# A float32r block kernel: weights of the gate and up products as the stationary operand

## What is computed

```python
def rmsnorm(x, g):
    xf = x.astype(jnp.float32)
    y = xf * lax.rsqrt(jnp.mean(xf * xf, axis=-1, keepdims=True) + EPS)
    return (y * g.astype(jnp.float32)).astype(x.dtype)

def swiglu(x, w_gate, w_up, w_down):
    return (jax.nn.silu(x @ w_gate) * (x @ w_up)) @ w_down

x = x + 0.5 * swiglu(rmsnorm(x, ffn1_norm[l]), ffn1_w_gate[l], ffn1_w_up[l], ffn1_w_down[l])
```

## Time and profile before

| | |
|---|---|
| median of 3 runs | 1442.88 us (1442.66 to 1445.46) |
| profiled execution, from its first to its last instruction (span) | 1440.0 us |
| mean granted TensorE clock | 0.985 |
| busy share of the span: TensorE, ScalarE, VectorE, POOL | 96%, 48%, 44%, 42% |
| HBM read | 240.16 MB, 168 GB/s over the span |

### The profile page before, as it was taken

The page is one execution under the profiler, slowest core; times in us unless marked ns, Lnnn a source line. Parts: engine busy times, 40 slices in busy tenths (PEclk is TensorE's granted clock), DMA queues, the critical chain, the costliest instruction groups (busy, mean ns, idle before and its releaser), DMA issues.

```text
span 1440.0 us, 16607 instructions
## 1 busy us (share of the span) xinstructions
PE 1387.0 (96%) x6628; PEld 1155.5 (80%) x6628; DVE 634.1 (44%) x715; ACT 690.4 (48%) x848; POOL 601.5 (42%) x208
## 2 busy tenths in 40 slices
PE   7999999898999999999999998899999999999997
PEld 5888887797788887888888787678888888888885
DVE  3333336655433335333335669865234421433333
ACT  5444446424444435444346683357543654644442
POOL 3443351634244434443532345544453432433442
PEclk9999999999999999999999999999999999999999
DMA  9555553312455554555553554245664453555550
GB/s 339 184 175 189 176 188 104 104 59 92 163 196 178 175 176 175 205 175 187 207 190 121 206 193 157 88 141 166 217 236 173 144 181 117 169 198 191 186 175 30
DMA packets 37217, 242.16 MB, mean 168 GB/s; under 512 B 5632, under 2 KB 6176, under 8 KB 9120
## 3 DMA queue, kind: packets, MB, share of 16 engines
q1 hardware_dynamic: 35264, 234.18, 47.5%
q10 hardware_dynamic: 1888, 7.07, 1.3%
HBM read 240.16 MB, written 1.08 MB: 168 GB/s over the span
## 4 chain that ended last, share of the span: by engine, by line
PE 88%; DVE 7%; ACT 2%; issue 2%; POOL 1%; DMA 0%; POOLq 0%; SPq 0%; DVEq 0%; ACTq 0%
PE acc L310 26%; PE acc L312 26%; PE acc L311 26%; PE work L849 3%; DVE mix L2153 2%; PE work L786 2%; PE work L483 1%; PE work L332 1%; DVE mix L2163 1%; DVE wlo L291 1%; ACT junk L344 1%; PE work L1633 1%; PE work L2362 0%; PE work L2337 0%; PE work L794 0%
## 5 line engine op out<-in xcount | busy, mean ns | idle before, releaser
L291 POOL TENSOR_TENSOR wlo<-raw,whi 128x2048 fp32r<-128x2048 f32 (+1 forms) x112 | 526.1, 4701 | 706.8 <-ACT whi L286 706.6
L310 PE MATMUL acc<-whi,xT_hi 128*128 128x512 f32 x1152 | 464.2, 403 | 9.3 <-DVE xT_lo L371 4.7
L286 ACT ACTIVATE whi<-raw 128x2048 fp32r<-128x2048 f32 (+1 forms) x223 | 417.9, 1886 | 91.0 <-PE acc L312 86.0
L312 PE MATMUL acc<-whi,xT_lo 128*128 128x512 f32 x1152 | 452.6, 393 | 0.0
L311 PE MATMUL acc<-wlo,xT_hi 128*128 128x512 f32 x1152 | 452.4, 393 | 0.0
L291 DVE TENSOR_TENSOR wlo<-raw,whi 128x2048 fp32r<-128x2048 f32 x111 | 293.0, 2640 | 243.5 <-ACT whi L286 239.9
L310 PEld LDWEIGHTS acc<-whi,xT_hi 128*128 128x128 f32 x1152 | 219.0, 190 | 55.8 <-issue 9.0
L312 PEld LDWEIGHTS acc<-whi,xT_lo 128*128 128x128 f32 x1152 | 218.5, 190 | 47.1
L311 PEld LDWEIGHTS acc<-wlo,xT_hi 128*128 128x128 f32 x1152 | 219.2, 190 | 42.2 <-issue 0.2
L310 PE MATMUL acc<-whi,hid_hi 128*128 128x512 f32 x352 | 137.6, 391 | 0.0
L312 PE MATMUL acc<-whi,hid_lo 128*128 128x512 f32 x352 | 137.1, 389 | 0.0
(11 more groups left out here) (356 smaller groups left out, 1367.5 us busy)
## 6 DMA issues: line engine op xcount, KB each, us to landing
raw<-in_t_ffn_up SPq DMA_DIRECT2D x87, 1024.0 KB, 4.9
raw<-in_t_m_in SPq DMA_DIRECT2D x52, 1024.0 KB, 5.0
raw<-in_t_ffn_down SPq DMA_DIRECT2D x40, 1024.0 KB, 4.9
raw<-in_t_m_os SPq DMA_DIRECT2D x8, 1024.0 KB, 4.9
raw<-in_t_xa_kv SPq DMA_DIRECT2D x8, 1024.0 KB, 5.0
raw<-in_t_ffn_down SPq DMA_DIRECT2D x8, 512.0 KB, 3.6
raw<-in_t_m_out SPq DMA_DIRECT2D x4, 1024.0 KB, 5.0
sum_rows<-row_scratch ACTq DMA_DIRECT2D x4, 1024.0 KB, 6.1
```

What stands on the lines that cost most here:

```text
L286: act.activation(granule(whi, u, i), granule(raw, u, i), ACT.Copy).then_inc(hi_ready, 1)
L291: eng.tensor_tensor(granule(wlo, u, i), granule(raw, u, i), granule(whi, u, i).bitcast(F32), ALU.subtract).then_inc(lo_odd if g % 2 else l ...
L310: pe.matmul(banks[t][:, 0:u.n], xhi[:, kt, tok], hi[:, j, :], start=first, stop=False)
L312: mm = pe.matmul(banks[t][:, 0:u.n], xlo[:, kt, tok], hi[:, j, :], start=False, stop=last)
```

## The change

The gate and up products swap their operands. A block j (22 per FFN) is 128 gate and 128 up columns with all eight k tiles, which is one granule; the host lays the weights out so. The weight tile of 128 x 128 is stationary, the 256 tokens move. The product comes out with features on the partitions, so the transposes of the hidden tile go away. The norm's scale now varies along the free dimension, so it can't be a per-partition scale any more: it is spread to a row on all partitions (`rstd_row`) with two diagonal tiles and matmuls with `ones`, and VectorE multiplies the gate by it ahead of the Silu. The scale of the up product is left to the end: the residual is scaled by `rstd_half`, half of `rstd`, in place of 0.5. All engines step by block instead of by unit, and the start of an FFN is written anew (`first_ups`). Cut to its core:

```diff
@@ plan_stream
-            add(f"ffn{f}.up{c}")
+            add(f"ffn{f}.up{c}", [tuple(range(KD))] * 2, 2 * P)
@@ residual_half
-            st = dve.scalar_tensor_tensor(out=x[:, t, c], in0=banks[t], scalar=alpha, in1=x[:, t, c],
+            scale = rstd_half[:, t:t + 1] if alpha is None else alpha
+            st = dve.scalar_tensor_tensor(out=x[:, t, c], in0=banks[t], scalar=scale, in1=x[:, t, c],
@@ reciprocal_rms
+            if b in FFN_NORM:
+                link(pool, pool.tensor_tensor(rstd[:, :], ms[:, :], minus_half[:, 0:NT], ALU.pow))
+                pool.tensor_scalar(rstd_half[:, :], rstd[:, :], 0.5, None, ALU.mult).then_inc(rstd_ready, 1)
@@ ffn_tensor
-        up(0, after_k={2 if b == B_FFN2 else 1: second_half}, halfway=lambda: pe.wait_ge(xlo_done, 2 * b + 2))
-        up(1, halfway=lambda: ffn_hidden_t(pe, f, 0))
-        up(2, halfway=lambda: ffn_hidden_t(pe, f, 1))
+        def products(j, part, kts, start, stop, it=None):
+            u, i = up_unit(f, j)
+            hi, lo = granule(whi, u, i), granule(wlo, u, i)
+            cols, out = slice(part * P, (part + 1) * P), up_bank(f, j)[:, part * T:(part + 1) * T]
+            for kt in kts:
+                pe.matmul(out, hi[:, kt, cols], xT_hi[:, kt, :], start=start and kt == kts[0], stop=False)
+                pe.matmul(out, hi[:, kt, cols], xT_lo[:, kt, :], start=False, stop=False)
+                mm = pe.matmul(out, lo[:, kt, cols], xT_hi[:, kt, :], start=False, stop=stop and kt == kts[-1])
+            return mm
+        def up(j, it=None):
+            n = BLOCKS * f + j
+            u, i = up_unit(f, j)
+            if j >= 4:
+                wait(pe, h_done, n - 3, it, 4)
+            wait_lo(pe, u.g + i, it)
+            products(j, 0, range(KD), True, True, it)
+            products(j, 1, range(KD), True, True, it).then_inc(gran_done, 1)
+        def first_ups():
+            near, far = range(KD // 2), range(KD // 2, KD)
+            u = up_unit(f, 0)[0]
+            pe.wait_ge(xlo_done, 2 * b + 1)
+            if f == 0:
+                pe.wait_ge(S["first_lo"], 1)
+            else:
+                wait_lo(pe, u.g)
+            products(0, 0, near, True, False)
+            if b != B_FFN2:
+                transpose_x(pe, b, 1)
+            if f:
+                wait_lo(pe, u.g + 1)
+                products(1, 0, near, True, False)
+            else:
+                wait_lo(pe, 0)
+            if b == B_FFN2:
+                transpose_x(pe, b, 1)
+            pe.wait_ge(xlo_done, 2 * b + 2)
+            products(0, 0, far, False, True)
+            products(0, 1, range(KD), True, True).then_inc(gran_done, 1)
...
+        def rstd_sums():
+            pe.wait_ge(diag_ready, NT * (f + 1))
+            for t in range(NT):
+                mm = pe.matmul(work[:, 0, t * P:(t + 1) * P], ones[:, :], rstd_diag[:, t, :], start=True, stop=True)
+            mm.then_inc(rows_summed, 1)
+        first_ups()
+        rstd_sums()
+        up(2)
+        up(3)
@@ ffn_scalar
+        def silu(j, it=None):
+            n = BLOCKS * f + j
+            wait(act, gate_scaled, n + 1, it, 4)
+            if n >= 2:
+                wait(act, h_done, n - 1, it, 4)
+            act.activation(gate_act[:, j % 2, :], gate_in[:, j % 2, :], ACT.Silu).then_inc(silu_done, 1)
+        def step(j, it=None):
+            silu(j - 1, it)
+            if j + 2 < BLOCKS:
+                split_hi(act, *up_unit(f, j + 2), it)
+            else:
+                split_hi(act, down[(j + 2 - BLOCKS) // 2], j % 2)
+            round_hidden(j - 1, it)
-        split_hi(act, units[f"ffn{f}.up1"], 0)
-        split_hi(act, units[f"ffn{f}.up1"], 1)
+        if b:
+            split_hi(act, *up_unit(f, 2))
         act.wait_ge(rstd_ready, b + 1)
@@ ffn_vector
+        def scale_gate(j, it=None):
+            u, i = up_unit(f, j)
+            wait(dve, gran_done, u.g + i + 1, it, RING)
+            dve.tensor_tensor(gate_in[:, j % 2, :], up_bank(f, j)[:, 0:T], rstd_row[:, :],
+                              ALU.mult).then_inc(gate_scaled, 1)
+        def step(j, it=None):
+            scale_gate(j - 1, it)
+            if j % 2 == 0 and j + 2 < BLOCKS:
+                split_lo(dve, *up_unit(f, j + 2), it)
+            elif j % 2 == 0:
+                split_lo(dve, down[(j + 2 - BLOCKS) // 2], 0)
+            product(j - 1, it)
+            rest_hidden(j - 1, it)
+        def spread_rstd():
+            dve.wait_ge(rstd_ready, b + 1)
+            for t in range(NT):
+                dve.tensor_scalar(rstd_diag[:, t, :], ident[:, :], rstd[:, t:t + 1], None,
+                                  ALU.mult).then_inc(diag_ready, 1)
+            dve.wait_ge(rows_summed, f + 1)
+            dve.tensor_copy(rstd_row[:, :], work[:, 0, 0:T]).then_inc(row_ready, 1)
+            dve.wait_ge(row_ready, f + 1)
         rest_xt(dve, b, 1)
-        split_lo(dve, units[f"ffn{f}.up1"], 0)
+        split_lo(dve, *up_unit(f, 2))
+        spread_rstd()
```

More of the change, by code:

```diff
@@ L68, in plan_stream, with add @@
     full = [(0, 1, 2, 3), (4, 5, 6, 7)]
-    def add(name, granules=full):
-        units[name] = Unit(name, granules, count[0])
+    def add(name, granules=full, n=512):
+        units[name] = Unit(name, granules, count[0], n)
         count[0] += len(granules)
@@ L451, in up @@
                 else:
-                    load(sp, units[f"ffn{f}.up{c}"], i, tile, it)
+                    u = units[f"ffn{f}.up{c}"]
+                    load_granule(sp, u.g + i, tile[:, i * SLOT:(i + 1) * SLOT], it)
         up(0)
@@ L472, in ffn_banks, with up_bank @@
         return pair((c + ffn_off[f]) % 2)
[L474 to L485, removed]
+    def up_bank(f, j):
+        return ffn_banks(f, j // 2)[j % 2]
@@ L487, in ffn_tensor, with up_unit @@
+    def up_unit(f, j):
+        return units[f"ffn{f}.up{j // 2}"], j % 2
     def ffn_tensor(pe, f):
         b = FFN_NORM[f]
[L490 to L498, removed]
@@ L511, in ffn_tensor @@
-        up(9, halfway=lambda: ffn_hidden_t(pe, f, 8))
-        up(10, halfway=lambda: ffn_hidden_t(pe, f, 9))
+            for j in range(4, 8):
+                up(j, it)
+        up(20)
+        up(21)
         for half in range(2):
             banks = ffn_banks(f, NCH + half)
-            if half == 0:
-                pe.wait_ge(h_done, 2 * (NCH * f + 10))
-            else:
-                pe.wait_ge(h_done, 2 * (NCH * f + 11))
+            pe.wait_ge(h_done, BLOCKS * f + 20 + 2 * half)
@@ L603, in ffn_vector @@
         b = FFN_NORM[f]
-        def product(c, it=None):
-            n = NCH * f + c
-            if n >= 2:
-                wait(dve, hidt_done, n - 1, it, 2)
-            for t in range(NT):
-                wait(dve, silu_done, 2 * n + t + 1, it, 4)
-                dve.scalar_tensor_tensor(out=hidden[:, c % 2, t, :], in0=ffn_banks(f, c)[t][:, CH:2 * CH],
-                                         scalar=rstd[:, t:t + 1], in1=gate_act[:, t, :],
-                                         op0=ALU.mult, op1=ALU.mult).then_inc(h_done, 1)
@@ new lines, in product, with rest_hidden @@
+        def product(j, it=None):
+            n = BLOCKS * f + j
+            wait(dve, silu_done, n + 1, it, 4)
+            dve.tensor_tensor(hidden[:, j % 2, :], up_bank(f, j)[:, T:2 * T], gate_act[:, j % 2, :],
+                              ALU.mult).then_inc(h_done, 1)
+        def rest_hidden(j, it=None):
+            n = BLOCKS * f + j
+            wait(dve, hidhi_done, n + 1, it, 4)
+            at = slice(j, j + 1) if it is None else bass.ds(it * 4 + j, 1)
+            flat = "p k t -> p (k t)"
+            dve.tensor_tensor(hid_lo[:, at, :].rearrange(flat), hidden[:, j % 2, :],
+                              hid_hi[:, at, :].rearrange(flat).bitcast(F32), ALU.subtract).then_inc(hidlo_done, 1)
@@ L628, in ffn_vector @@
         rest_xt(dve, b, 1)
-        split_lo(dve, units[f"ffn{f}.up1"], 0)
+        split_lo(dve, *up_unit(f, 2))
+        spread_rstd()
         step(1)
         step(2)
+        step(3)
         with dve.Fori(0, TURNS) as it:
-            step(3, it)
-            step(4, it)
-        step(9)
-        down = [units[f"ffn{f}.down{half}.{j}"] for half in range(2) for j in range(3)] + next_units
-        product(9)
-        split_lo(dve, down[0], 0)
-        rest_hidden(9)
-        product(10)
-        split_lo(dve, down[1], 0)
@@ L642, in ffn_vector @@
-        rest_hidden(10)
+            for j in range(4, 8):
+                step(j, it)
+        step(20)
+        step(21)
+        step(22)
         split_lo(dve, down[2], 0)
         split_lo(dve, down[3], 0)
-        residual(dve, b + 1, 0, down[2], ffn_banks(f, NCH), 0.5)
+        residual(dve, b + 1, 0, down[2], ffn_banks(f, NCH), None)
         if b + 1 == B_FFN2:
```

132 lines of the change are left out of this document (52 added, 80 removed).

## The result

The kernel after takes **1586.99 us** (median of 4, 1585.75 to 1588.46) against 1444.17 of the kernel before beside it (1442.66 to 1445.68). The ratio is 1.0985, 95% interval 1.0972 to 1.0999: 142.8 us slower. The forecast was 1449 with a range to 1478. The direction was right, the size was not, and no rival reached this time; the highest stood at 1476.

The account below looks back on a forecast made before the run. TensorE, busy 96% of 1440.0 us, was taken as the bound. Terms 0 - 19.8 + 0.9 + 11.2 + 2.6 + 10.4 = +5.3 gave 1445.3 profiled, 1448.2 for runs, stated as 1449 for idle-time risk; range 1439 to 1478.

Parts of the forecast that it names:

- The matmuls: Gate and up products on TensorE: 4224 matmuls at 0.1135 us, surcharge over 2.4 GHz growing with columns; term 0.
- The rival with a fixed price per matmul: TensorE's gate and up products: 13.7 ns on each matmul whatever its width, 0.1204 us, +29, giving 1476; chance 0.24.
- The pace at the load floor: Rival for TensorE's gate and up matmuls: 0.1117 us each, the weight load's limit, giving 1440.6, no slowdown; chance 0.12.
- the 109 ns of the Trainium skill's formula: Rival for TensorE's 256-column matmuls: N/2.4 + 2.5 ns, a term of -19, giving 1430; chance 0.06.
- The transposes: Transposes of hidden on TensorE go away: 44 groups of four at 0.45 us, -19.8.
- Off the path: Loads, VectorE, ScalarE and POOL stay hidden: VectorE and ScalarE's two-block loop takes 10.5 us against TensorE's 10.9.
- One of its rivals: VectorE and ScalarE's loop becomes the bound (11.2 us, +11) or the clock falls; about 1456 to 1460, chance 0.13.
- The waits at block 3: TensorE waits for POOL's low weights once per FFN: 2.8 us (+11.2 in all), 4.1 in the first and fourth.
- the table load's share: In the first and fourth FFN the Silu loads its table, 1.28 us, begun when its input is there: +2.6.
- The starts: Start of each FFN: TensorE has less to multiply before waiting; +1.7, +3.0, +2.7, +3.0 by FFN, together +10.4.
- the sums' 0.9: Norm scale: TensorE's matmuls with ones, 8 in all, with the handover on the path: +0.9.
- a stop of 2.9 us leaves the clock alone: TensorE's granted clock kept 1.00 after a 2.9 us stop, but was 0.50 for 6.8 us after one of 4.4.

Follow-up runs that it names:

- experiment 3: Kernel before with 256 unread float32r matmuls of eight widths added at the end; starts 226.7 ns apart at 512 columns, 119.8 at 256; kernel time means nothing.
- experiment 8: Kernel before with three of the four transposes of each hidden tile left out; 1429.22 us, ratio 0.9890.
- experiment 5: Kernel after, hidden tile left in SBUF, with ScalarE rounding each granule of weights one block earlier; 1470.22 us, ratio 1.0186 to the kernel before.
- Experiment 6: Kernel after with VectorE taking all subtractions of the gate and up blocks instead of POOL; 1539.37 us, ratio 1.0656 to the kernel before.
- experiment 1: Kernel after with the hidden tile moved from SBUF to PSUM; 1489.58 us, ratio 1.0311 to the kernel before.
- Experiment 4: Kernel after with the hidden tile in PSUM and ScalarE rounding each granule of weights one block earlier; 1472.20 us, ratio 1.0194 to the kernel before.
- experiment 7: Kernel of Experiment 4 with 24 instead of 12 matmuls per block, gate and up, ahead of the second half of x; 1468.25 us, ratio 1.0161.

## Why the prediction was right or wrong

**The matmuls: the term was mis-sized, 0 where it is +26.** The prediction took the surcharge as growing with the columns, since the 8- and 32-column durations differ by just their columns. They lie under the floor of 111 ns (experiment 3), which the prediction puts down to the weight load, so a fixed price can't show in them. The prediction said as much in a bracket and then weighed them anyway. The rival with a fixed price per matmul, at 0.24, had the mechanism and the size: 0.1204 forecast, 0.120 measured. The pace at the load floor (0.1117) and the 109 ns of the Trainium skill's formula are both refuted.

**The transposes: right.** -19.8 forecast, -21.4 estimated from experiment 8.

**Off the path: the step that failed.** It put the ring of VectorE and ScalarE at 10.5 us for two blocks against 10.9 on TensorE and costed it at nothing. It summed durations by width from rows in which POOL did not stand in the way, and did not ask where the inputs lie. In the kernel before the same subtraction reads its minuend from `work`, in PSUM; the change takes the transposes away, and with them that PSUM tile, and leaves an instruction with both inputs in SBUF next to an engine that reads SBUF for 4.6 us in every 13.9. The forecast's ring less its eleven handovers of 0.05, which the rows don't show (the next instruction starts about when the one before ends), is 9.9 us; with 4.0 for the held L655 it is 13.9. "SBUF — State Buffer" of the Trainium skill (section "SBUF: two separate sides") has the rule: VectorE and GpSimd share a pair of ports, a lock and no split of bandwidth, which a VectorE instruction with two SBUF inputs needs against a GpSimd instruction that reads SBUF, and the later one waits for the whole of the other. The trace agrees: 0.43 us or 4.46 for the same instruction, 44 of 44 held until POOL's ends. The trace of the kernel before had it too, in VectorE's own subtraction of weights, both of whose inputs lie in SBUF:

```profile
L291 DVE TENSOR_TENSOR wlo<-raw,whi x111: 2279/2293/6575, 23.2 to 1408.1; 128x2048 fp32r<-128x2048 f32 x111
```

Sixteen of the 111 took 3 us or more, all beside a POOL instruction. The prediction used the shortest, 2.29, named the mean, 2.64, and did not ask what lies between them. One of its rivals named the ring as a bound, but priced its overrun at 0.3 us a pair, and it is 2.4.

How much is it? The kernel after and the one of experiment 5 differ by 1586.99 - 1470.22 = 116.8 us, their profiled spans by 118.2. From the first matmul of block 2 to the last of block 21, ten pairs of blocks, the four FFNs take 140.5, 139.8, 139.5 and 140.8 us in the kernel after, a ring of 14.0 each time, and 115.15 each in experiment 5. That is 100 us. The starts differ by 1.4 the other way. The 20 that are left fall behind block 21; in 9.8 of them the down product waits for POOL's low weights, and the rest was not followed.

The same sum by what TensorE does: its waits for POOL's low weights are 74.3 + 9.8 in the one and 5.7 in the other:

```profile
PE acc L498 <- DVE xT_lo L373: 9.6, 3, 4.2
PE acc L498 <- POOL wlo L299: 5.7, 2, 2.9
```

That is 78 us. Then the granted clock: its mean is 0.957 over 1586.6 us and 0.977 over 1468.4, so 68.2 against 33.8 us of full clock not granted, 34 more. Two blocks each of the kernel after, one stretch with the clock at 1.00 and one in which it fell, and the wait that lies in the first:

```profile
100.00:113.30 13.30, 12.62 (x105) 12.44 (x105) 7.96 (x7) 5.16 (x6) 4.60 (x1) 1.00 0.46 158
113.30:127.30 14.00, 11.76 (x86) 11.58 (x85) 8.71 (x8) 5.17 (x6) 4.56 (x1) 0.88 0.46 150
```

```profile
108.70 0.36 PE L498 MATMUL acc<-xT_hi,whi 128*128 128x256 f32 x1 [0.68 <-POOL wlo L299]
```

78 + 34 = 112 of 117. The two are not separate losses in the blocks. Where the clock fell after a wait, TensorE did the next blocks later, and the next wait was 0.7 us instead of 2.2: at 108.70, after a fall from 96.15 to 99.56, and again at 136.61, after one from 123.45 to 126.87. The ring took 13.9 to 14.1 either way. So the ring sets the time, and the slow stretches lie inside its slack. Experiment 6 bears on the clock too: there 71 waits, none over 1.1 us, went with a mean of 0.977.

**The waits at block 3: right.** 2.8 and 4.1 us were forecast; experiment 1, in which the ring doesn't cover them, shows 2.4 to 2.7 in the second and third FFN and 3.7 in the first and fourth, with the table load's share. Experiment 4 removes them and gains 17.4, more than their 12.5; in experiment 1 the clock fell behind the first and the last of them, and in experiment 4 it doesn't.

**The starts: the mechanism right, the size short.** From the first product to block 2 (unit 1 before) the four FFNs take 14.6, 12.1, 13.8 and 12.1 us in the kernel before, 52.7 in all, and 18.6, 17.5, 20.2 and 16.0 in that of experiment 5, 72.2. Of the 19.5 us, 11.3 were forecast (10.4 and the sums' 0.9) and 2.5 are the pace. What is left, 5.7, goes with half clock: the fourth FFN, whose start stayed at 1.00 throughout, takes 3.9 us more than before, just what the forecast and the pace give, and the excess lies in the other three. Windows of the kernel of experiment 5, the second and the third FFN:

```profile
383.00:389.80 6.80, 3.97 (x32) 3.57 (x31) 3.01 (x7) 5.55 (x10) 5.58 (x4) 1.00 0.31 88
389.80:393.20 3.40, 3.40 (x18) 3.40 (x18) 3.20 (x2) 1.96 (x2) 1.59 (x2) 0.50 0.81 289
...
584.40:591.20 6.80, 6.23 (x29) 6.23 (x30) 4.17 (x4) 5.96 (x8) 5.20 (x8) 0.50 0.09 13
```

After a stop of 2.8 us the clock was at its lower level for 3.40 us, and in the third FFN for 6.80. The prediction took from the earlier trace rows that a stop of 2.9 us leaves the clock alone. That row was one case, not a bound. The second and the fourth FFN of this very kernel have the same stop, and only after the first of these two did the clock fall:

```profile
388.56 0.39 PE L498 MATMUL acc<-xT_hi,whi 128*128 128x256 f32 x1 [2.83 <-POOL wlo L299]
```

```profile
1271.97 0.39 PE L498 MATMUL acc<-xT_hi,whi 128*128 128x256 f32 x1 [2.86 <-POOL wlo L299]
```

**The books.** From the kernel before to the one of experiment 5: +25.7 for the pace, -21.4 for the transposes, +17 for the starts without their pace, 21 in sum, and 24.9 measured; the 4 us left over are not assigned. From there to the kernel after: 116.8 for the ring, with the waits at block 3, the clock and the 20 us behind block 21 in it.

**Is there a version that wins?** The best of these, experiment 7, is 23 us above the kernel before. The swap by itself earns 21.4 and pays 25.7, so even with no stop added it would not win as it stands. Streaming both parts of x as 512 columns past one weight tile would, by the measured widths, take 227 + 120 instead of 3 x 120 ns per k tile and part, 18 us less in all, an estimate, but needs twice the PSUM and additional sums on VectorE. This was not tried.

## What to carry to other kernels

When an edit moves a tile from PSUM to SBUF, look again at every VectorE instruction that reads it: price it by what POOL does at that moment, not by its width. Sum the handovers between two engines as a ring and compare it with the bound engine's period; if the margin is smaller than one unsure duration, the ring is the forecast's largest risk, and moving one link a step earlier (here one rounding) is the cheap cure. And take a price per instruction only from rows in which no other floor lies above it.

## What was not expected of the hardware

- A float32r matmul costs its columns at 2.4 GHz and some 13 ns on top (226.7 ns at 512, 119.8 at 256; up to 16 between), with a floor of 111 ns at 192 and 128 columns, measured with an fp32 weight tile loaded for each.
- A 128x256 VectorE subtraction with both inputs in SBUF took 0.42 us or up to 4.64, the end of POOL's 4.6 us subtraction deciding; with one input in PSUM 88 of 88 took 0.425. A multiplication of a 128x128 tile by a scale per partition, with one large input, was held in the same way, 4.6 us in place of 0.28, in three of four FFNs of experiments 4, 5 and 7.
- Stops of 2.0 to 2.8 us were followed by a granted clock of 0.50 in some places (389.80 in experiment 5, behind a stop of 2.83) and not in others (a stop of 2.86 at 1271.97 of the same run); what else decides is open.
